# A fused two-block transformer on one core: the forget gate of the second block's attention computed in another layout

## What is computed

```python
log_f = log_sigmoid(f_logit + b_forget)        # f_logit [tokens, 8] = rms_norm(x) @ w_in[:, 6144:6152]
c = cumsum(log_f, over tokens)
sc = q @ k.T * scale + c[query] - c[key]       # per head, masked where key > query
p = softmax(sc); out = p @ v
```

## Time and profile before

| | |
|---|---|
| median of 3 runs | 2896.45 us (2892.68 to 2897.11) |
| profiled execution | 2894.63 us |
| its span | 2893.0 us, 42703 instructions |
| granted TensorE clock | 0.999 |

### The profile page before, as it was taken

The page is one execution under the profiler, slowest core; times in us unless marked ns, Lnnn a source line. Parts: engine busy times, 40 slices in busy tenths (PEclk is TensorE's granted clock), DMA queues, the critical chain, the costliest instruction groups (busy, mean ns, idle before and its releaser), DMA issues.

```text
span 2893.0 us, 42703 instructions
## 1 busy us (share of the span) xinstructions
PE 2860.5 (99%) x15684; PEld 2398.0 (83%) x15684; DVE 1878.4 (65%) x3402; ACT 1330.5 (46%) x2044; POOL 102.9 (4%) x162
## 2 busy tenths in 40 slices
PE   8999999999999999999999999999999999999998
PEld 6778787777788788888877888888888888888887
DVE  3378686764577646776886666667876556565566
ACT  3343333333333534544556545455655445354455
POOL 0000000101000000111000000000000000000000
PEclk9999999999999999999999999999999999999999
DMA  9954444443456234433545444444555555545555
GB/s 377 356 194 178 174 161 170 179 172 151 153 220 226 103 112 142 158 133 146 185 160 181 168 163 173 166 169 167 184 189 202 189 189 190 197 180 202 182 197 189
DMA packets 77804, 529.61 MB, mean 183 GB/s; under 512 B 9264, under 2 KB 11568, under 8 KB 15056
## 3 DMA queue, kind: packets, MB, share of 16 engines
q1 hardware_dynamic: 73872, 515.95, 48.8%
q0 software_dynamic: 2912, 9.57, 1.0%
q10 hardware_dynamic: 864, 1.94, 0.2%
HBM read 525.31 MB, written 2.11 MB: 182 GB/s over the span
## 4 chain that ended last, share of the span: by engine, by line
PE 95%; DMA 2%; DVE 2%; ACT 1%; issue 1%; POOL 0%; ACTq 0%; POOLq 0%; DVEq 0%
PE bank L1999 28%; PE bank L2002 14%; PE bank L1989 9%; PE bank L1991 9%; PE bank L1990 9%; PE bank L2408 4%; PE bank L2409 4%; PE bank L2410 4%; PE bank L2035 2%; PE bank L2036 2%; PE bank L2037 2%; PE bank L2218 1%; DMA raw<-stream 1%; PE bank L2177 1%; PE bank L2048 1%; PE bank L2102 1%
## 5 line engine op out<-in xcount | busy, mean ns | idle before, releaser
L1169 DVE TENSOR_TENSOR w_lo<-raw,w_hi 128x1024 fp32r<-128x1024 f32 x784 | 948.1, 1223 | 464.8 <-ACT w_hi L657 461.9
L657 ACT ACTIVATE w_hi<-raw 128x1024 fp32r<-128x1024 f32 x784 | 824.4, 1057 | 669.7 <-DMA raw<-stream 212.6
L1989 PE MATMUL bank<-x,w_hi 128*128 128x512 f32 x1120 | 442.8, 395 | 3.0 <-issue 1.8
L1991 PE MATMUL bank<-x,w_lo 128*128 128x512 f32 x1120 | 436.3, 390 | 0.0
L1990 PE MATMUL bank<-x,w_hi 128*128 128x512 f32 x1120 | 436.1, 389 | 0.0
L670 ACT ACTIVATE z<-bank 128x512 f32<-128x512 f32 x256 | 153.2, 599 | 483.2 <-PE bank L2002 310.7
L1999 PE MATMUL bank<-xs,w_hi 128*128 128x512 f32 x1184 | 304.7, 397 | 0.0
L1989 PEld LDWEIGHTS bank<-x,w_hi 128*128 128x128 f32 x1120 | 210.3, 188 | 70.1 <-issue 26.0
L1999 PE MATMUL bank<-mlp_x,w_hi 128*128 128x512 f32 x1024 | 257.1, 393 | 0.0
L1991 PEld LDWEIGHTS bank<-x,w_lo 128*128 128x128 f32 x1120 | 210.2, 188 | 44.5
L1999 PEld LDWEIGHTS bank<-xs,w_hi 128*128 128x128 f32 x1184 | 213.0, 189 | 39.9 <-DVE xs L1279 1.1
(11 more groups left out here) (349 smaller groups left out, 3624.3 us busy)
## 6 DMA issues: line engine op xcount, KB each, us to landing
raw<-stream SPq DMA_DIRECT2D x488, 1024.0 KB, 4.8
res<-tokens POOLq DMA_DIRECT2D x8, 512.0 KB, 8.9
work<-tokens POOLq DMA_DIRECT2D x16, 256.0 KB, 3.1
res<-cond_rows SPq DMA_DIRECT2D x8, 256.0 KB, 4.1
out<-res SPq DMA_DIRECT2D x8, 256.0 KB, 2.4
gain_sb<-final_gain ACTq DMA_DIRECT2D x1, 1024.0 KB, 7.0
table_sb<-tables ACTq DMA_DIRECT2D x1, 640.0 KB, 3.5
pool_sb<-pool_w POOLq DMA_DIRECT2D x8, 64.0 KB, 2.2
```

The source lines that it names most:

```text
L657: own.inc(act.activation(w_hi[:, 2 * unit.parity + g, :], raw[:, unit.slot, g * HALF:(g + 1) * HALF], ACT.Copy), hi_done, 2 * unit.number ...
L1169: own.inc(dve.tensor_tensor(w_lo[:, n, :], raw[:, unit.slot, g * HALF:(g + 1) * HALF], w_hi[:, n, :].bitcast(F32), ALU.subtract), lo_done, ...
L1989: pe.matmul(bank[:, :], hi, tile(k)[:, 0, :], start=k == 0, stop=False)
L1991: ins = pe.matmul(bank[:, :], lo, tile(k)[:, 0, :], start=False, stop=k == KT - 1)
```

## The change

The logits are made from plain float32 weights (times the norm's gain, on VectorE at tile 9 of the second output projection) and plain float32 activations: tile k goes to column strip k mod 4 (32 partitions of the result), four products at a time behind tiles 3, 7, 11 and 15. ScalarE copies the strips (in its queue behind the squares); two products with a chooser matrix add the four strips and bring tokens to partitions (behind L2318). Bias, log-sigmoid and root are then applied to 128 partitions x 16. After value unit 14 five products make the running sums of all heads, once with tokens on partitions and once with heads on 8 partitions; VectorE scales both in its queue between the roundings of units 15 and 16. GpSimd writes the latter to DRAM, reads it back with eight broadcasts to 128 partitions (128 KB each), and adds the mask to the late half. In the heads L2332, L2339 to L2341, L2362, L2364, L1748, L1751 and L1766 go; VectorE adds the key bias in L1783's place, with one more add of 128x128.

```diff
+        wf_pad = place("wf_pad", [KT, SQUARE], F32, shared_at + 5120)
...
+        bias_low = place("bias_low", [HEADS // 2, TOK], F32, q_at + 4 * D // 2)
+        bias = [bias_low[:, p, :] if p < HEADS // 2 else work[:, p - HEADS // 2, TOK:WIDE] for p in range(HEADS)]
+        cum_dram = nc.dram_tensor("cum_rows", (HEADS, TOK), F32, kind="Internal").ap()
...
+        gate_strips = a_t[:, 0, TOK:WIDE]
+        cum_rows = a_t[0:HEADS, 2, TOK:WIDE]
...
             norm_roots(1)
+            pool.wait_ge(cum_in, 1)
+            pool.dma_start(cum_dram, cum_rows).then_inc(cum_out, 16)
+            pool.wait_ge(cum_out, 16)
+            for p in range(HEADS):
+                pool.dma_start(bias[p], cum_dram[p:p + 1, :].rearrange("h t -> (h t)").partition_broadcast(P)).then_inc(bias_in, 16)
+            pool.wait_ge(bias_in, 16 * HEADS)
+            for p in range(HEADS):
+                own.inc(pool.tensor_tensor(bias[p][:, P:TOK], bias[p][:, P:TOK], table_sb[:, 3, P:TOK], ALU.add), bias_full, p + 1)
             for t in range(2):
...
             layer_out(1)
-            act.wait_ge(table_in, 32)
-            act.activation(wf_hi[:], wf_raw[:], ACT.Copy).then_inc(f_hi, 1)
             norm(1, TOK)
...
                 square_tile(k)
+            act.wait_ge(f_mm, 1)
+            act.activation(gate_strips, att[3][:, 0:TOK], ACT.Copy).then_inc(strips_in, 1)
             split(Unit(W_IN2 + 9))
...
             act.wait_ge(f_in, 1)
-            own.inc_own(act.activation(gate_rows, gate_rows, ACT.Exp, scale=-1.0))
+            own.inc_own(act.activation(gate_f[:], gate_f[:], ACT.Exp, scale=-1.0))
             own.wait_own()
-            own.inc(act.activation(gate_rows, gate_rows, ACT.Ln, bias=one[0:HEADS, :]), f_exp, 1)
+            own.inc(act.activation(gate_f[:], gate_f[:], ACT.Ln, bias=one), f_exp, 1)
             split(Unit(W_IN2 + 13))
...
                             fold_affine()
+                        if l == 1 and k == 9:
+                            gate_weights()
                     if l == 0:
...
+            def gate_weights():
+
+                dve.wait_ge(table_in, 32)
+                own.inc_own(dve.memset(wf_pad[:], 0.0))
+                own.wait_own()
+                for k in range(KT):
+                    last = dve.tensor_scalar(wf_pad[:, k, 0:HEADS], wf_raw[:, k, :], vcol("norm_mix_g", k), None, ALU.mult)
+                own.inc(last, f_weights, 1)
+
             def fold_affine():
...
             layer_out(1)
-            dve.wait_ge(f_hi, 1)
-            own.inc(dve.tensor_tensor(wf_lo[:], wf_raw[:], wf_hi[:].bitcast(F32), ALU.subtract), f_lo, 1)
             norm(1, TOK)
...
             own.inc(dve.tensor_copy(mix_rms, att[1][:, TOK:TOK + 2]), mix_in, 1)
+            own.wait_own()
+            b_forget = vec[:, VEC_COLS["b_forget"]:VEC_COLS["b_forget"] + HEADS]
+            dve.wait_ge(f_cols, 1)
             split(Unit(W_IN2 + 12))
-            dve.wait_ge(f_mm, 1)
-            own.inc_own(dve.tensor_copy(gate_rows, att[3][0:HEADS, TOK:WIDE]))
+            for t in range(2):
+                stt(log_f[:, t, :], att[3][:, TOK + HEADS * t:TOK + HEADS * (t + 1)], mix_rms[:, t:t + 1], b_forget, ALU.mult, ALU.add)
             own.wait_own()
-            tt(log_rows, att[3][0:HEADS, 0:TOK], gate_rows, ALU.add)
+            ts(gate_f[:], log_f[:], -1.0, ALU.mult)
             own.wait_own()
-            tt(log_rows, log_rows, rms_mix[0:HEADS, :], ALU.mult)
+            own.inc(dve.tensor_tensor(gate_f[:], gate_f[:], log_f[:], ALU.max), f_in, 1)
             own.wait_own()
-            ts(log_rows, log_rows, vcol("b_forget", 0)[0:HEADS, :], ALU.add)
-            own.wait_own()
-            ts(gate_rows, log_rows, -1.0, ALU.mult)
-            own.wait_own()
-            own.inc(dve.tensor_tensor(gate_rows, gate_rows, log_rows, ALU.max), f_in, 1)
-            own.wait_own()
-            ts(log_rows, log_rows, 0.0, ALU.min)
+            ts(log_f[:], log_f[:], 0.0, ALU.min)
             dve.wait_ge(f_exp, 1)
             own.wait_own()
-            own.inc(dve.tensor_tensor(log_rows, log_rows, gate_rows, ALU.subtract), f_full, 1)
+            own.inc(dve.tensor_tensor(log_f[:], log_f[:], gate_f[:], ALU.subtract), f_full, 1)
...
                 split(Unit(W_IN2 + n))
+                if n == 15:
+                    dve.wait_ge(cum_mm, 1)
+                    own.inc(dve.tensor_scalar(cum_rows, att[3][0:HEADS, 0:TOK], -1.0 / HEAD_SCALE, None, ALU.mult), cum_in, 1)
+                    ts(cum_f[:], att[3][:, TOK:TOK + 2 * HEADS].rearrange("p (t h) -> p t h", t=2), 1.0 / HEAD_SCALE, ALU.mult)
...
                     def before():
-                        if kind == "qb":
-
-                            dve.wait_ge(lf_done, p + 1)
-                            own.inc_own(dve.tensor_copy(log_f[:], att[4][:, TOK:TOK + 2]))
-                            own.wait_own()
-                            for t in range(2):
-                                last = dve.tensor_scalar(log_b[:, t, :], table_sb[:, 4, P:2 * P],
-                                                         log_f[:, t:t + 1], -1.0 / HEAD_SCALE, ALU.mult, ALU.mult)
-                            own.inc(last, lb_full, p + 1)
-                        elif kind in ("kb", "ga1"):
+                        if kind in ("kb", "ga1"):
...
...
-                        elif kind == "ga0":
-                            dve.wait_ge(f_cum, p + 1)
-                            ts(cum_f[:], att[4][:, TOK + 2:TOK + 4], 1.0 / HEAD_SCALE, ALU.mult)
                         elif kind == "gb0":
...
                                 else:
-                                    stt(w, sc, cum_f[:, t:t + 1], table_sb[:, 2 + t, 0:keys], ALU.add, ALU.add)
+                                    if t == 0:
+                                        dve.wait_ge(bias_full, p + 1)
+                                    stt(w, sc, cum_f[:, t, p:p + 1], bias[p] if t else table_sb[:, 2, 0:P], ALU.add, ALU.add)
+                            if c == 1:
+                                own.wait_own()
+                                tt(work[:, 2, 0:P], work[:, 2, 0:P], bias[p][:, 0:P], ALU.add)
                             own.wait_own()
...
-                if k == 0:
-                    pe.wait_ge(f_lo, 1)
-                pe.matmul(att[3][0:HEADS, :].rearrange("p (a t) -> p a t", a=2), wf_hi[:, k, :], xs[:, k, :, :],
-                          start=k == 0, stop=False)
-                ins = pe.matmul(att[3][0:HEADS, 0:TOK], wf_lo[:, k, :], xs[:, k, 0, :], start=False, stop=k == KT - 1)
+                if k % 4 < 3:
+                    return
+                if k == 3:
+                    pe.wait_ge(f_weights, 1)
+                for j in range(4):
+                    ins = pe.matmul(att[3][SQUARE * j:SQUARE * (j + 1), 0:TOK], wf_pad[:, k - 3 + j, :], res[:, k - 3 + j, 0:TOK],
+                                    start=k == 3, stop=k == KT - 1)
                 if k == KT - 1:
                     ins.then_inc(f_mm, 1)
+
+            def forget_columns():
+
+                pe.wait_ge(strips_in, 1)
+                for t in range(2):
+                    ins = pe.matmul(att[3][:, TOK + HEADS * t:TOK + HEADS * (t + 1)], gate_strips[:, P * t:P * (t + 1)], chooser[:],
+                                    start=True, stop=True)
+                ins.then_inc(f_cols, 1)
+
+            def forget_sums():
+
+                pe.wait_ge(f_full, 1)
+                late, full = att[3][:, TOK + HEADS:TOK + 2 * HEADS], table_sb[:, 4, :]
+                pe.matmul(att[3][:, TOK:TOK + HEADS], full[:, 0:P], log_f[:, 0, :], start=True, stop=True)
+                pe.matmul(late, full[:, P:TOK], log_f[:, 0, :], start=True, stop=False)
+                pe.matmul(late, full[:, 0:P], log_f[:, 1, :], start=False, stop=True)
+                pe.matmul(att[3][0:HEADS, 0:TOK], log_f[:, 0, :], full, start=True, stop=False)
+                pe.matmul(att[3][0:HEADS, P:TOK], log_f[:, 1, :], full[:, 0:P], start=False, stop=True).then_inc(cum_mm, 1)
...
                     ins.then_inc(mix_mm, 1)
+                    forget_columns()
+                if n == 14:
+                    forget_sums()
...
                     product(unit, "narrow", 4, xs)
-                    if kind == "ka":
-
-                        pe.wait_ge(f_full, 1)
-                        pe.wait_ge(v_out, 16 + 8)
-                        pe.wait_ge(z_used, unit.taken)
-                        for t in range(2):
-                            ins = pe.matmul(att[4][:, TOK + t:TOK + t + 1], log_rows[:, P * t:P * (t + 1)],
-                                            ident[0:HEADS, p:p + 1], start=True, stop=True)
-                        ins.then_inc(lf_done, 1)
-                    elif kind == "kb":
-
-                        pe.wait_ge(lb_full, p + 1)
-                        o = att[4][:, TOK + 2:TOK + 4]
-                        pe.matmul(o[:, 0:1], table_sb[:, 4, 0:P], log_f[:, 0:1], start=True, stop=True)
```

(52 more changed lines are left out.)

## The result

The changed kernel takes 2875.72 us in the median (2875.33 to 2876.49, 4 runs), the kernel before 2894.56 us on the same chip (2892.05 to 2897.11): a ratio of 0.9933, 95% interval 0.9921 to 0.9945. The forecast was 2875.5 us. The profiled execution took 2876.09 us.

What follows compares the result with a forecast made beforehand. TensorE, busy 99% of the span, was taken to bound the kernel. Terms of -17.8, -2.4, -1.4, +0.45 and +1.3 sum to -19.85 us; forecast 2875.5 us, own range 2870 to 2881, stretched to 2884 for a rival.

Steps and rivals of the forecast that it cites:

- Heads: Eight heads: one-column, running-sum and bias products leave TensorE's queue, 2.23 us per head, 17.8 us less in all.
- Logits: Second output projection: old product pairs go (5.5 us), four strip groups come (3.1 us), net -2.4 us, bounds -3.8 and +2.8.
- rival without overlap: Logits: strip products run one after the other, records 0.22 us apart, +5.2 us, 2880.7 us; chance 0.03.
- Stall: Value unit 13: TensorE's wait for w_lo goes as the gate's logarithm steps end 2.2 us earlier, -1.4 us.
- Column products and running sums: Values stage, TensorE: two added column products cost +0.45 us, five products for running sums +1.3 us, bounds 0.9 to 1.6.
- Weights times gain: VectorE at tile 9, second output projection: up to 3.5 us of added work, hidden in its idle time; nothing, bound +1.
- Bias through DRAM: GpSimd's write, broadcasts and adds take 12 us (10.6 to 33), hidden before head 0's third softmax, some 24 to spare.
- rival (d): Head 0: broadcasts land one after another, bias comes late, TensorE stops; 77 us late, 2952 us; chance 0.03.
- Rival (c): GpSimd's eight adds hold up VectorE's roundings one for one: 0 to +7.7 us, up to 2883; chance 0.04.
- Rival (e): Value unit 13: last step still waits or a new wait replaces it, 2876 to 2877 us; within the forecast's 0.85.

Runs made afterwards that it cites:

- experiment 4: Changed kernel with the products dropped from TensorE's heads put back as products nobody reads, VectorE's old part left out: 2893.03 us.
- experiment 3: Changed kernel with all 16 logit products in one group after tile 15, four of one strip before the next strip's: 2877.60 us.
- Experiment 7: Changed kernel with six VectorE steps on 8 partitions x 256 put ahead of the gate's logarithm steps: 2876.93 us.
- experiment 8: Changed kernel with the memset and 16 small gate-weight products after tile 15 of the second output projection instead of tile 9: 2875.67 us.
- experiment 6: Changed kernel with the eight bias broadcasts issued and awaited five times over, 2889.79 us, or four times over, 2880.92 us in one run.
- experiment 9: Changed kernel with 96 more unread GpSimd adds of 128x256 behind its eight; no median given, TensorE lost 3.4 us.

## Why the prediction was right

*Heads, -17.8.* Measured -18.17, 2.27 a head against 2.23, and experiment 4 puts 18.1 back with TensorE's products alone. Reading start to start, and never durations, is what made this term good: the rows of the bias products in experiment 4 have 0.39 + 0.82 = 1.21 us for what costs 0.87.

*Logits, -2.4.* Measured -1.98: the groups cost 0.77 (forecast 0.78), so the miss of 0.4 is in what went, 5.1 us instead of 5.5: a pair of the old products cost 0.37 on the average of the tiles, where the forecast had read 0.39 from one, and the first group of tiles gave 0.1 less, where the changed kernel waits 0.8 us for operand tiles and the kernel before 0.4. The rival without overlap would have shown 0.22 us between neighbouring records where the trace has 0.006; experiment 3 shows that the loops' order decides on it.

*Stall, -1.4.* Measured -1.39. The last step starts 2.4 us earlier against TensorE's products, where 2.2 were forecast and 1.4 needed. Experiment 7 brings the wait back. The forecast told it by VectorE's last step; what released VectorE's rounding was ScalarE's, which the forecast had only as next in line and moving along.

*Column products and running sums, +0.45 and +1.3.* Measured +0.47 and +1.50. The second is within its bounds of 0.9 to 1.6; the tenth after the group was not counted.

*Weights times gain, nothing.* 2.7 us of work (forecast up to 3.5), and the norm was not later. With no cover it is 1.1 us at most (experiment 8), in line with the prediction's bound of +1.

*Bias through DRAM, hidden.* 12.7 us from the write to the first add (forecast 12), with 22.3 + 4.3 us to spare (forecast 24 + 5). That 12 is near is partly luck: its lower bound of 10.6 had 2.1 us for the last landing, and the broadcasts land after some 6 us; it had 0.64 for an issue, and they come every 0.54 us; and 12 was set above the bound without a row. They land side by side, not one after the other; rival (d) had its place and its slope right (experiment 6) and its premise wrong.

*Rival (c).* The mutual hindrance is real already in the changed kernel: beside the eight adds VectorE took 1.52 us for a rounding, 0.69 for a sum and 0.57 for a product, 0.7 us more in all than their usual 1.22, 0.43 and 0.43. It lies in slack; 114 us of adds, where the change has 5.1, were needed to make 3.4 us of it (experiment 9).

*Rival (e).* No new wait took the stall's place: TensorE is busy in 57.00 of the 57 us from 1540 to 1597.

The terms measured sum to -19.6 (forecast -19.85), and the single profiled pair shows 18.5 because the changed kernel's execution had 6.8 us of half clock at the norms and the other 3.4, less 0.7 us of start-up, which differs by a us or two from run to run. The medians differ by 18.8, 21.0 and 19.0 us in the three sets of runs. That the median came within 0.3 us of the forecast is partly luck: the kernel before had 2896.45 in the runs that the forecast started from and 2894.56 in those of the result.

## What to carry to other kernels

When one engine is busy in every microsecond of a stage, price a change in that stage by that engine's start-to-start times, and check for each other engine only how late it may become: such a room was a fixed number here (35 us) that cost nothing up to its end and one for one behind it, plus what the clock took for the stop. Work that depends on data known early for all heads pays when it is done once, off that engine, even through DRAM. And small products on column strips should go round the strips, since neighbours on one strip started 0.216 us apart here and neighbours on different strips 0.006.

## What the runs showed of the hardware that was not expected

Strip after strip, products did not run fully one by one: after five records alone, two strips overlapped, 4.53 us in place of the 7.0 forecast and the 1.86 of the round-robin order.

A VectorE step of 128x256 with two SBUF operands took 0.3 us longer beside GpSimd's adds (425 to 722 ns), one with a PSUM source no longer (418 and 414 ns).

The granted clock dropped to half at a norm in every profiled execution, for 3.4 or 6.8 us. The three executions of the changed kernel had it at layer 0, at layer 1 and at both.
